# Weights times values in stick-breaking attention: three split products per head against one fp32 product on half of the array

## The chip, the cores and the metric

The kernel runs on one core of a Trainium2 chip. The metric is the device time of one execution in microseconds. Time before: median of three runs 3162.48 us (3160.17 to 3165.97).

## The reference

One step of a two-layer encoder: layer 0 uses latent attention, layer 1 stick-breaking attention, each followed by a squared-ReLU MLP. There are 1024 prompt frames, and 8 streams of 16 new frames with 128 cached ones. All tensors are fp32. What the change touches is the second mixer:

```
def sb_attend(q, q_pos, k, v, k_pos):
    z = einsum('bqhd,bkhd->bhqk', q, k) * (SB_HEAD_DIM ** -0.5)
    mask = (k_pos[None, :] < q_pos[:, None])
    log_keep = where(mask, log_sigmoid(-z), 0.0)
    suffix = cumsum(log_keep, axis=3, reverse=True) - log_keep
    a = where(mask, exp(log_sigmoid(z) + suffix), 0.0)
    return einsum('bhqk,bkhd->bqhd', a, v)

def sb_mixer(h, ...):            # 16 heads of 64
    qkv = (h @ w_in).reshape(B, S, 3, 16, 64)
    q, k, v = qkv[:, :, 0], qkv[:, :, 1], qkv[:, :, 2]
    out = attend_queries(sb_attend, ...)
    return out.reshape(B, S, 1024) @ w_o, k, v     # k and v are outputs too
```

## The kernel before, in words

**Number formats.** A product that must be exact is mostly made of three fp32r matmuls: each operand is split into a high part (a copy cast to fp32r) and a low part (the rest), and `product` (lines 72 to 76) issues high x high, high x low and low x high. [...]

**Stages.** Latent attention, MLP 0, `sb_input_stage` (projection to q, k, v; tiles named d_), `sb_attention_stage` (tiles named e_), then MLP 1. The change touches the two sb stages.

**sb_input_stage.** 60 tasks of 24 matmuls. For a v task of the prompt ScalarE casts the high half (L1770) and copies the rows for the output `new_p_sb_v` (L1776), VectorE makes the low half (L1805), and SyncE stores the rows (L1697) and both halves to the scratch tensor `sb_v` (L1712). Three tasks after the k tasks end, SyncE loads the operands of the first pair of heads (`load_queries_keys`, 12 transfers, `load_values`, 4 transfers).

**sb_attention_stage.** Heads go in 8 pairs, two pairs (32 steps) to a loop body: three passes of a hardware loop (`Fori`) and one written out. A step is one query tile of 128 rows of one head; `where(n)` gives pair, head and query tile. The order in a pair is q0, q1 of head 0, q0, q1 of head 1, then q2, q3 of each, and so on. Four steps are a group, two steps (one head) a unit. The chain of a step with q+1 key tiles:

- TensorE, `scores`: keys times queries, one or two chunks of up to 512 columns in four PSUM banks (L2301), and the mask (L2304).
- ScalarE, `weights`: two sigmoids of each chunk (L2101, L2103).
- VectorE, `scan`: a running product from the right (L2240). It frees the score bank.
- GpSimd, `weigh`: sigmoid times scan (L2190), the weights `take` (e_b).
- TensorE, `transposes`: each 128x128 block of weights is turned (L2357), up to four to a task, into one of three PSUM banks.
- ScalarE, `transposed_hi`: casts a task to the high part in `pt` (L2130); then VectorE, `transposed_lo`: writes the rest (L2272) and so frees the bank (`t_lo`).
- TensorE, `values`: after each unit, for each key tile, three matmuls of 256 columns into bank 7 (L74, L75, L76). The stationary operand holds the 64 value columns of the head beside 64 columns of zeros, so both heads of a pair add into one 128x256 result: head 0 fills partitions 0 to 63, head 1 the others.
- ScalarE, `output`: copies the result (L2137), SyncE stores it.

`pt` is two buffers of a high and a low part, one for each unit in turn. The order on each engine is the order of the code; all waits are on semaphores. On TensorE body step n runs a piece of the sample streams' attention if n+1 is odd (L2311 to L2336), `scores(n+4)`, `transposes(n+1)`, and, if n is odd, `values`. A task bank may be filled again when `emptied` holds. At the start of the stage VectorE zeroes parts of `pt` (L2222) and the 64 zero columns in each of the four value tiles (L2228); TensorE waits for all twelve of these (`const_done`).

Of the kernel before, what the change touches and what calls it, by code (L numbers as in the profile page):

```python
# [37 lines left out]
P = 128  # L38
# [1517 lines left out]
def sb_operands(nc, ctx, name):  # L1556

    q = ctx.enter_context(nc.sbuf_tensor(f"{name}_q", [P, 2, SEQ], F32R))
    k = [ctx.enter_context(nc.sbuf_tensor(f"{name}_k{s}", [P, 2, SEQ], F32R)) for s in "hl"]
    v = [ctx.enter_context(nc.sbuf_tensor(f"{name}_v{s}", [P, NPT, 3 * SB_DIM], F32R)) for s in "hl"]  # L1560
    return q, k, v


QK_LOADS, V_LOADS = 12, 4
# [17 lines left out]
def load_values(sp, scratch, operands, p, done):  # L1582

    for s in range(2):
        for a in range(2):
            sp.dma_start(f32(operands[2][s][:, :, 2 * a * SB_DIM:(2 * a + 1) * SB_DIM]),
                         scratch["sb_v"][s].rearrange("(t p) n -> p t n", p=P)[
                             :, :, bass.ds(p * 2 * SB_DIM + a * SB_DIM, SB_DIM)]).then_inc(done, 16)


def sb_input_stage(nc, io, scratch, h_t, sample):
# [22 lines left out]
    def to_halves(n):  # L1614

        kind, _, t = TASKS[n]
        return kind == "q" or (kind == "v" and t < NPT)
# [19 lines left out]
    with nc.cleanup_on_exit(), ExitStack() as ctx:  # L1637
# [45 lines left out]
        def _(sp):  # L1683
# [15 lines left out]
            def store_halves(n):  # L1699
                kind, g, t = TASKS[n]  # L1700
                for s in range(2):
# [4 lines left out]
                    elif kind == "k":  # L1706
# [3 lines left out]
                    else:  # L1710
                        dst = scratch["sb_v"][s, t * P:(t + 1) * P, (g - 4) * WIDTH:(g - 3) * WIDTH]
# [4 lines left out]
            for n in range(N):  # L1716
# [12 lines left out]
                if n == PRELOAD_AT:  # L1729
                    for u in range(3):  # L1730
                        half_stored[u].wait(sp, 32 * count(halves_stored, LAST, u))
                    done.wait(sp, LAST)
                    load_queries_keys(sp, scratch, first_pair, 0, first_in.sem)
                    load_values(sp, scratch, first_pair, 0, first_in.sem)
# [3 lines left out]
            first_in.wait(sp, 16 * (QK_LOADS + V_LOADS))  # L1738

        @block.scalar  # L1740
        def _(act):
# [19 lines left out]
            for n in range(N):  # L1761
# [5 lines left out]
                if to_halves(n):  # L1767
                    half_stored[n % 3].wait(act, 32 * count(halves_stored, n, n % 3))
                    width = COLS if kind == "q" else WIDTH
                    act.copy(half_st[n % 3][0][:, 0:width], task_bank(n)[:, 0:width]).then_inc(hi_out.sem, 1)  # L1770
# [22 lines left out]
        def _(dve):  # L1793
            for piece in range(0, PIECES, 2):
                weights_rest(dve, piece)
            for n in range(N):
                kind, g, t = TASKS[n]
                hi, lo = (x[:, 0:COLS if kind == "q" else WIDTH] for x in half_st[n % 3])
                if to_halves(n):
# [3 lines left out]
                    if to_rows(n):  # L1803
                        rows_out.wait(dve, count(to_rows, n + 1))
# [126 lines left out]
def sb_attention_stage(nc, io, scratch, first_pair, sample):  # L1931
# [7 lines left out]
    TURNS = S.count(TASKS, "prompt")  # L1939
# [3 lines left out]
    with nc.cleanup_on_exit(), ExitStack() as ctx:  # L1943
# [9 lines left out]
        pt = [[sb(f"e_pt{u}{s}", [P, NPT, GQ], F32R) for s in "hl"] for u in range(2)]  # L1953
        take = [sb("e_b0", [P, SEQ])]
        sample_rows(nc, ctx, "e")
        sb_operands(nc, ctx, "e_first")
        take += [sb(f"e_b{u}", [P, SEQ]) for u in range(1, 4)]
# [22 lines left out]
        t_done, t_hi, t_lo = signal("e_t"), signal("e_t_hi"), signal("e_t_lo", 3)  # L1980
# [24 lines left out]
        def emptied(pe, i, m):  # L2005
# [3 lines left out]
            if kind == "prompt":  # L2009
                t_lo.wait(pe, TURNS * i + S.count(before + 1, "prompt"))  # L2010
            elif kind == "values":
                smp_o.wait(pe, 2 * (S.SAMPLE_STEPS * i + S.count(before + 1, "values")))
            else:
                smp_out.wait(pe, 3 * S.SAMPLE_STEPS * i + S.count(before + 1, "keys", "scores", "turn"))

# [6 lines left out]
        def batch(i, f):  # L2022
            return 2 * i + f // 2

# [9 lines left out]
        def _(sp):  # L2034
# [22 lines left out]
            def body(i, last):  # L2057
                load_cache_k(i, 1, 2 * i + 1)
                for pair in range(2):
                    for g in range(4):  # L2060
# [5 lines left out]
                        if g == 0 and not (last and pair == 1):  # L2066
# [3 lines left out]
                            pv_done.wait(sp, S.UNITS * i + S.UNITS // 2 * pair)  # L2070
                            load_values(sp, scratch, operands[1 - pair], 2 * i + pair + 1, v_in.sem)
# [8 lines left out]
            sp.sem_inc(v_in.sem, 16 * V_LOADS)  # L2080
# [9 lines left out]
        def _(act):  # L2090
            o_done.start(act)
            smp_out.start(act)

# [24 lines left out]
            def transposed_hi(i, n):  # L2118
                unit, at = n // 2, (n % 2) * P
                for j, (kind, task) in enumerate(S.tasks(n)):  # L2120
                    m = S.before(n) + j
                    if kind == "values":
                        continue
# [4 lines left out]
                    pv_done.wait(act, S.UNITS * i + unit - 1)  # L2128
                    s0 = task[0][1]
                    act.copy(pt[unit % 2][0][:, s0:s0 + len(task), at:at + P],  # L2130
# [363 lines left out]
```

## Time and profile before

| | |
|---|---|
| median of three runs | 3162.48 us (3160.17 to 3165.97) |
| the profiled execution | 3161.52 us, span 3159.8 us |
| mean granted TensorE clock | 0.972 of full speed |
| busy: PE, DVE, ACT, POOL | 94%, 39%, 31%, 20% of the span |
| sb_input_stage | to about 1802 us |
| sb_attention_stage | about 1802 to 2225 us |

TensorE (PE) is the busiest engine nearly everywhere. [...] PEld is the load of the stationary operand, a record of its own.

### The profile page before, as it was taken

The page shows a single profiled execution, that of the slowest core. Times are in us where ns is not written, and L with a number is a line of the kernel's source. Part 1 is how long each engine was busy: PE and PEld are TensorE (multiplying, and loading weights), DVE is VectorE, ACT ScalarE, POOL GpSimd, SP SyncE. Part 2 cuts the span into 40 slices and gives each one's busy share as a digit, 9 for nine tenths or more (in the row PEclk, how much of TensorE's full clock was granted, in tenths as well). Part 3 has the DMA queues.
Part 4 walks back from the last instruction along what each step waited for, and adds up shares of the span by engine and source line. Part 5 has one row for each costly group of instructions (what it writes and reads, how often), then busy time and mean ns, then how long its engine had stood idle before and what let it go on. Part 6 is the DMA issues. An engine that isn't in the chain of part 4 may idle for free. (4 is left out here: it accounts for less than half of the span.)

```text
span 3159.8 us, 43537 instructions
## 1 busy us (share of the span) xinstructions
PE 2973.8 (94%) x16067; PEld 2648.4 (84%) x16067; DVE 1240.2 (39%) x1945; ACT 980.8 (31%) x2003; POOL 632.3 (20%) x484
## 2 busy tenths in 40 slices
PE   7979996999999999998999898899799999999998
PEld 6868885788999989997988777787679998899987
DVE  5556661442333323334101176767333332233324
ACT  4334442321122111223122265666322221122212
POOL 3100000121222112211121144444112211122111
PEclk9989997999999999999999999999899999999999
DMA  4211103411111111111345563643401111111111
GB/s 138 84 43 42 40 29 91 168 35 40 40 53 46 36 37 40 53 40 59 122 147 182 174 137 87 136 97 68 142 10 51 53 46 33 40 40 53 46 34 74
DMA packets 216173, 227.82 MB, mean 72 GB/s; under 512 B 50688, under 2 KB 174080, under 8 KB 216064
## 3 DMA queue, kind: packets, MB, share of 16 engines
q1 hardware_dynamic: 216064, 226.41, 24.5%
q8 instruction: 63, 1.03, 0.1%
q14 instruction: 46, 0.38, 0.0%
HBM read 170.36 MB, written 56.00 MB: 72 GB/s over the span
## 5 line engine op out<-in xcount | busy, mean ns | idle before, releaser
L1449 DVE TENSOR_TENSOR x<-m_ps,x 128x512 f32<-128x512 f32 x324 | 224.0, 691 | 670.4 <-PE m_ps L76 670.4
L1484 DVE TENSOR_TENSOR m_sq<-m_relu 128x384 f32<-128x384 f32 x192 | 171.1, 891 | 524.8 <-ACT m_relu L1388 524.8
L74 PE MATMUL m_ps<-h_h,m_up0h 128*128 128x384 f32 x768 | 258.8, 337 | 8.2 <-POOL m_up0l L1422 8.2
L75 PE MATMUL m_ps<-h_l,m_up0h 128*128 128x384 f32 x768 | 258.3, 336 | 0.0
L76 PE MATMUL m_ps<-h_h,m_up0l 128*128 128x384 f32 x768 | 258.3, 336 | 0.0
L74 PE MATMUL m_ps<-h_h,m_up1h 128*128 128x384 f32 x768 | 256.5, 334 | 0.0
L75 PE MATMUL m_ps<-h_l,m_up1h 128*128 128x384 f32 x768 | 256.5, 334 | 0.0
L76 PE MATMUL m_ps<-h_h,m_up1l 128*128 128x384 f32 x768 | 256.5, 334 | 0.0
L1388 ACT ACTIVATE m_relu<-m_ps 128x384 f32<-128x384 f32 x192 | 94.5, 492 | 513.9 <-PE m_ps L76 513.8
L2190 POOL TENSOR_TENSOR e_b<-e_b,e_r 128x128 f32<-128x128 f32 (+7 forms) x128 | 155.1, 1215 | 224.9 <-DVE e_r L2240 218.5
L1383 ACT CAST m_dn0h<-m_dn_raw 128x1024 fp32r<-128x1024 f32 x16 | 16.8, 1051 | 548.2 <-PE m_ps L76 548.2
L74 PEld LDWEIGHTS m_ps<-h_h,m_up0h 128*128 128x128 f32 x768 | 145.5, 190 | 9.2 <-POOL m_up0l L1422 8.6
L75 PEld LDWEIGHTS m_ps<-h_l,m_up0h 128*128 128x128 f32 x768 | 145.5, 189 | 0.5
L76 PEld LDWEIGHTS m_ps<-h_h,m_up0l 128*128 128x128 f32 x768 | 145.4, 189 | 0.0
L1429 POOL TENSOR_TENSOR m_dn0l<-m_dn_raw,m_dn0h 128x1024 fp32r<-128x1024 f32 x16 | 38.6, 2410 | 529.3 <-ACT m_dn0h L1383 529.3
L74 PEld LDWEIGHTS m_ps<-h_h,m_up1h 128*128 128x128 f32 x768 | 144.2, 188 | 0.0
L75 PEld LDWEIGHTS m_ps<-h_l,m_up1h 128*128 128x128 f32 x768 | 144.2, 188 | 0.0
L76 PEld LDWEIGHTS m_ps<-h_h,m_up1l 128*128 128x128 f32 x768 | 144.2, 188 | 0.0
L1422 POOL TENSOR_TENSOR m_up0l<-m_up_raw,m_up0h 128x1024 fp32r<-128x1024 f32 x32 | 76.7, 2396 | 320.2 <-ACT m_up0h L1376 320.2
L1488 DVE TENSOR_TENSOR m_ul<-m_sq,m_uh 128x384 fp32r<-128x384 f32 x192 | 113.2, 590 | 18.1
L1422 POOL TENSOR_TENSOR m_up1l<-m_up_raw,m_up1h 128x1024 fp32r<-128x1024 f32 x32 | 76.8, 2400 | 209.0 <-ACT m_up1h L1376 209.0
L2240 DVE TENSOR_TENSOR_SCAN e_r<-e_ps,e_zero 128x256 f32<-128x256 f32 (+3 forms) x128 | 108.6, 849 | 20.6 <-ACT e_ps L2103 18.2
(511 smaller groups left out, 7747.3 us busy)
## 6 DMA issues: line engine op xcount, KB each, us to landing
m_up_raw<-in_mlp_w_up SPq DMA_DIRECT2D x64, 512.0 KB, 4.6
m_dn_raw<-in_mlp_w_down SPq DMA_DIRECT2D x64, 512.0 KB, 3.6
h_raw<-scratch_oT SPq DMA_DIRECT2D x4, 1536.0 KB, 15.4
scratch_qr<-a_qrst SPq DMA_DIRECT2D x9, 512.0 KB, 3.4
a_x<-in_x_prompt SPq DMA_DIRECT2D x8, 512.0 KB, 4.9
b_qr<-scratch_qr SPq DMA_DIRECT2D x4, 1024.0 KB, 6.9
scratch_oT<-b_o SPq DMA_DIRECT2D x32, 128.0 KB, 1.7
new_p_sb_k<-d_rows SPq DMA_DIRECT2D x16, 256.0 KB, 2.1
```

The costliest lines, as they stand in the source:

```text
L74: pe.matmul(out, w[0], m[0], start=start, stop=False)
L75: pe.matmul(out, w[0], m[1], start=False, stop=False)
L76: return pe.matmul(out, w[1], m[0], start=False, stop=stop)
L1383: act.copy(w_dn[j][0][:], dn_raw[:]).then_inc(dn_hi.sem, 1)
L1388: act.activation(relu[n % 2][:], bank[:, (n + 2) % 4, 0:GROUP], ACT.Relu).then_inc(relu_done.sem, 1)
L1422: pool.tensor_tensor(w_up[j % 2][1][:], up_raw[:], f32(w_up[j % 2][0][:]), ALU.subtract).then_inc(up_lo.sem, 1)
L1429: pool.tensor_tensor(w_dn[j][1][:], dn_raw[:], f32(w_dn[j][0][:]), ALU.subtract).then_inc(dn_lo.sem, 1)
L1449: dve.tensor_tensor(x[:, t, cols], bank[:, 4 + n % 3, :], x[:, t, cols], ALU.add).then_inc(added.sem, 1)
L1484: dve.tensor_tensor(sq[n % 2][:], relu[n % 2][:], relu[n % 2][:], ALU.mult).then_inc(sq_done.sem, 1)
L1488: dve.tensor_tensor(u_t[1][:, j, cols], sq[n % 2][:], f32(u_t[0][:, j, cols]), ALU.subtract).then_inc(u_lo.sem, 1)
L2190: pool.tensor_tensor(b, b, rest[n % 2][:, SEQ - used + 1:SEQ + 1], ALU.mult).then_inc(weighted.sem, 1)
L2240: dve.tensor_tensor_scan(rest[n % 2][:, at:at + used][:, ::-1], keep[:, 0:used][:, ::-1], zero[:].broadcast_to([P, used]), start, ALU.mult ...
```

## The change

`pt` becomes four plain fp32 buffers (a unit each, so two groups), without high and low part. Each transposed task is copied once, by ScalarE or by VectorE in turns over the tasks (`copier`). The values are one fp32 tile of the pair's 128 columns, loaded with one transfer straight from the output `new_p_sb_v`; the scratch tensor `sb_v`, its halves and the zero columns go. `values` runs once a group, in two halves around the transposes of a step; each key tile has two fp32 matmuls with 64 stationary columns, head 0 into partitions 0 to 63 of bank 7 and head 1 into partitions 64 to 127. ScalarE's `output` now comes behind its copies of the step.

```diff
 def load_values(...):
-    for s in range(2):
-        for a in range(2):
-            sp.dma_start(f32(operands[2][s][:, :, 2 * a * SB_DIM:(2 * a + 1) * SB_DIM]),
-                         scratch["sb_v"][s]...)
+    sp.dma_start(operands[2][:], io["new_p_sb_v"][0, 0].rearrange("(t p) h c -> p t (h c)", p=P)[
+        :, :, bass.ds(p * 2 * SB_DIM, 2 * SB_DIM)]).then_inc(done, 16)
 # sb_input_stage
     def to_halves(n):
-        return kind == "q" or (kind == "v" and t < NPT)
+        return TASKS[n][0] == "q"
 # sb_attention_stage
-        pt = [[sb(f"e_pt{u}{s}", [P, NPT, GQ], F32R) for s in "hl"] for u in range(2)]
+        pt = [sb(f"e_pt{u}", [P, NPT, GQ]) for u in range(4)]
+        def copier(m):
+            return S.count(m, "prompt") % 2
+        def turned_rows(n, task):
+            s0, at = task[0][1], (n % 2) * P
+            return pt[n // 2 % 4][:, s0:s0 + len(task), at:at + P]
 # ScalarE
-            def transposed_hi(i, n):
+            def transposed(i, n):
-                    if kind == "values":
+                    if kind == "values" or kind == "prompt" and copier(m) == 1:
                         continue
-                    act.copy(pt[unit % 2][0][:, s0:s0 + len(task), at:at + P], ...)
+                    pv_done.wait(act, S.GROUPS * i + n // 4 - 1)
+                    act.copy(turned_rows(n, task), turned_in(m, task)).then_inc(t_out[0].sem, 1)
 # VectorE
-            for x in (*v[0], *v[1]):
-                dve.memset(f32(x[:, :, SB_DIM:2 * SB_DIM]), 0.0).then_inc(const_done.sem, 1)
-                    t_hi.wait(dve, TURNS * i + S.count(m + 1, "prompt"))
-                    dve.tensor_tensor(lo, task_bank(m)..., f32(hi), ALU.subtract).then_inc(t_lo.sem, 1)
+                    if kind == "prompt" and copier(m) == 1:
+                        t_done.wait(dve, TASKS * i + m + 1)
+                        pv_done.wait(dve, S.GROUPS * i + n // 4 - 1)
+                        dve.tensor_copy(turned_rows(n, task), turned_in(m, task)).then_inc(t_out[1].sem, 1)
 # TensorE
-            def values(i, unit):
-                for k, slot in order:
-                    done = product(pe, bank[:, 7, 0:GQ],
-                                   [x[:, k, a * SB_DIM:a * SB_DIM + P] for x in v[pair]],
-                                   [x[:, slot, :] for x in pt[unit % 2]], ...)
+            def values(i, g, half):
+                if half == 0:
+                    for u in range(2):
+                        t_out[u].wait(pe, TURNS * i + copies(ready, u))
+                for k, slot in order[middle:] if half else order[:middle]:
+                    for a in range(2):
+                        rows = slice(a * SB_DIM, (a + 1) * SB_DIM)
+                        done = pe.matmul(bank[rows, 7, 0:GQ], v[pair][:, k, rows], pt[2 * (g % 2) + a][:, slot, :],
+                                         start=k == last_q, stop=k == last_q - 1)
             def body(i, last):
                 for n in range(S.STEPS):
-                    step(i, n + S.VALUES_LAG, last)
-                    if n % 2 == 1:
-                        values(i, n // 2)
+                    m = n + S.VALUES_LAG
+                    step(i, m, last)               # without the transposes
+                    if n % 4 == 3:
+                        values(i, n // 4, 0)
+                    if not (last and m >= S.STEPS):
+                        transposes(i, m)
+                    if n % 4 == 3:
+                        values(i, n // 4, 1)
```

TensorE, second group of the first pair, before: the end of the fifth step's transposes and the start of head 1's values (e_pt1h and e_pt1l are the two parts of the turned weights, d_first_vh and d_first_vl those of the values).

```order
L2301 MATMUL e_ps<-d_first_kh,d_first_q 128x512
L2301 MATMUL e_ps<-d_first_kl,d_first_q 128x512
L95 REGISTER_ALU
L2357 MATMUL e_ps<-ident,e_b 128x128 x4
L95 REGISTER_ALU
L2357 MATMUL e_ps<-ident,e_b 128x128
L74 MATMUL e_ps<-e_pt1h,d_first_vh 128x256
L75 MATMUL e_ps<-e_pt1l,d_first_vh 128x256
L76 MATMUL e_ps<-e_pt1h,d_first_vl 128x256
```

TensorE at the same place now.

```order
L2301 MATMUL e_ps<-d_first_kh,d_first_q 128x512
L2301 MATMUL e_ps<-d_first_kl,d_first_q 128x512
L95 REGISTER_ALU x2
L2376 MATMUL e_ps<-e_pt,d_first_v 64x256 x4
L95 REGISTER_ALU
L2357 MATMUL e_ps<-ident,e_b 128x128 x4
L95 REGISTER_ALU
L2357 MATMUL e_ps<-ident,e_b 128x128
L2376 MATMUL e_ps<-e_pt,d_first_v 64x256 x4
```

The first half of the values now stands ahead of the transposes, directly behind the scores; both heads' products for a key tile follow each other, and the values of head 0, which had stood two steps earlier, are in the same two blocks.

VectorE at two steps of five and six key tiles, before (e_r is the scan).

```order
L2240 SCALAR_TENSOR_TENSOR e_r<-e_ps,e_r,e_zero 128x512
L2272 TENSOR_TENSOR e_pt0l<-e_ps,e_pt0h 128x4x128
L2272 TENSOR_TENSOR e_pt0l<-e_ps,e_pt0h 128x128
L95 REGISTER_ALU
L2240 SCALAR_TENSOR_TENSOR e_r<-e_ps,e_zero 128x384
L95 REGISTER_ALU x2
L2240 SCALAR_TENSOR_TENSOR e_r<-e_ps,e_r,e_zero 128x512
L2272 TENSOR_TENSOR e_pt0l<-e_ps,e_pt0h 128x4x128
L2272 TENSOR_TENSOR e_pt0l<-e_ps,e_pt0h 128x2x128
```

VectorE at the same two steps now.

```order
L2244 SCALAR_TENSOR_TENSOR e_r<-e_ps,e_r,e_zero 128x512
L95 REGISTER_ALU x2
L2273 COPY e_pt<-e_ps 128x128
L95 REGISTER_ALU
L2244 SCALAR_TENSOR_TENSOR e_r<-e_ps,e_zero 128x384
L95 REGISTER_ALU x2
L2244 SCALAR_TENSOR_TENSOR e_r<-e_ps,e_r,e_zero 128x512
L95 REGISTER_ALU
L2273 COPY e_pt<-e_ps 128x2x128
```

VectorE has one copy a step in place of two subtractions; the tasks of four tiles of these two steps went to ScalarE alone.

## Rows read from the trace of the kernel before

**Rows 1.** The page: busy time of each engine, share of the span.

```profile
PE 2973.8 (94%) x16067; PEld 2648.4 (84%) x16067; DVE 1240.2 (39%) x1945; ACT 980.8 (31%) x2003; POOL 632.3 (20%) x484
```

**Rows 2.** Busy time by stretch, the attention stage: PE, PEld, DVE, ACT, POOL, clock, DMA.

```profile
1805.00:1905.00 100.00, 92.58 (x613) 78.59 (x613) 70.99 (x108) 66.90 (x176) 46.52 (x47) 0.92 0.51 116
...
2105.00:2218.00 113.00, 102.47 (x713) 87.67 (x711) 77.54 (x120) 70.72 (x184) 47.08 (x45) 0.96 0.27 64
sum 413.00, PE 376.51 PEld 321.91 DVE 283.67 ACT 264.12 POOL 180.33; mean PE 94.13 PEld 80.48 DVE 70.92 ACT 66.03 POOL 45.08
```

**Rows 3.** Groups of instructions by line: values, busy and mean ns, idle before.

```profile
L74 PE MATMUL e_ps<-e_pt1h,e_second_vh 128*128 128x256 f32 x80 | 25.8, 323 | 4.8 <-DVE e_pt1l L2272 4.8
...
L75 PE MATMUL e_ps<-e_pt0l,d_first_vh 128*128 128x256 f32 x80 | 22.6, 282 | 0.0
```

**Rows 4.** Timeline of PE: start us, duration us. Values at full clock.

```profile
2007.74 0.28 PE L76 MATMUL e_ps<-e_pt0h,e_second_vl 128*128 128x256 f32 x1
2007.86 0.28 PE L74 MATMUL e_ps<-e_pt0h,e_second_vh 128*128 128x256 f32 x1
2007.98 0.28 PE L75 MATMUL e_ps<-e_pt0l,e_second_vh 128*128 128x256 f32 x1
```

**Rows 5.** Timeline of PE: four plain fp32 calls of 144 columns, eight records.

```profile
1858.77 1.14 PE L2320 MATMUL e_ps<-e_kT,e_qz 128*128 128x144 f32 x8
```

**Rows 6.** Timeline of PE and PEld: stationary loads beside matmuls.

```profile
1874.05 0.28 PE L76 MATMUL e_ps<-e_pt0h,e_second_vl 128*128 128x256 f32 x1
1874.05 0.19 PEld L74 LDWEIGHTS e_ps<-e_pt0h,e_second_vh 128*128 128x128 f32 x1
1874.41 1.04 PEld L2320 LDWEIGHTS e_ps<-e_kT,e_qz 128*128 128x128 f32 x8
```

**Rows 7.** Timeline of PE: 16 stationary rows between 128, and 16 stationary columns between 128.

```profile
1866.26 0.40 PE L2336 MATMUL e_ps<-e_wT,e_nv 16*128 16x32 f32 x2
1866.59 0.41 PE L2335 MATMUL e_ps<-e_wT,e_cv 128*128 128x32 f32 x2
1866.93 0.40 PE L2336 MATMUL e_ps<-e_wT,e_nv 16*128 16x32 f32 x2
...
2001.28 0.27 PE L2327 MATMUL e_ps<-ident,e_bs 128*128 128x128 f32 x1
2001.39 0.27 PE L2328 MATMUL e_ps<-ident,e_bs 128*16 128x128 f32 x1
2001.42 0.36 PE L2301 MATMUL e_ps<-d_first_kh,d_first_q 128*128 128x256 f32 x1
2001.62 0.28 PE L2301 MATMUL e_ps<-d_first_kl,d_first_q 128*128 128x256 f32 x1
```

**Rows 8.** Waits of PE in the stage: us in total, times, longest.

```profile
PE e_ps L2301 <- DVE e_r L2240: 12.0, 18, 3.1
PE e_ps L2301 <- DVE e_second_vl L2228: 10.0, 1, 10.0
PE e_ps L74 <- DVE e_pt1l L2272: 7.3, 12, 1.4
PE e_ps L2357 <- DVE e_pt0l L2272: 5.8, 16, 1.0
PE e_ps L74 <- DVE e_pt0l L2272: 4.7, 10, 0.6
PE e_ps L2357 <- DVE e_pt1l L2272: 4.5, 7, 0.9
```

**Rows 9.** Timeline from the last store of the input stage to the first scores.

```profile
1797.16 0.62 SPq L1697 DMA_DIRECT2D new_s_sb_v<-d_rows  x1
1802.06 0.34 SPq L2045 DMA_DIRECT2D e_ck<-in_cache_sb_k  x1
...
1804.82 0.48 DVE L2228 MEMSET e_second_vl<- 128x512 f32 x1
1805.36 0.58 PE L2301 MATMUL e_ps<-d_first_kh,d_first_q 128*128 128x256 f32 x1 [9.99 <-DVE e_second_vl L2228]
```

**Rows 10.** Timeline: one task's cast and subtraction, two scans.

```profile
2194.09 1.21 DVE L2240 TENSOR_TENSOR_SCAN e_r<-e_ps,e_zero 128x512 f32<-128x512 f32 x1
2195.41 1.28 DVE L2240 TENSOR_TENSOR_SCAN e_r<-e_ps,e_r,e_zero 128x512 f32<-128x512 f32 x1
2216.31 0.59 ACT L2130 CAST e_pt1h<-e_ps 128x512 fp32r<-128x512 f32 x1 [5.78 <-PE e_ps L2357]
2216.93 0.69 DVE L2272 TENSOR_TENSOR e_pt1l<-e_ps,e_pt1h 128x512 fp32r<-128x512 f32 x1 [0.73 <-ACT e_pt1h L2130]
```

More of the change, by code:

```diff
@@ L1705, in store_halves @@
                         src = src[:, 0:COLS]
-                    elif kind == "k":
+                    else:
                         a = PAIRS_W * (g - 2)
@@ L1768, in _ @@
                     half_stored[n % 3].wait(act, 32 * count(halves_stored, n, n % 3))
-                    width = COLS if kind == "q" else WIDTH
-                    act.copy(half_st[n % 3][0][:, 0:width], task_bank(n)[:, 0:width]).then_inc(hi_out.sem, 1)
+                    act.copy(half_st[n % 3][0][:, 0:COLS], task_bank(n)[:, 0:COLS]).then_inc(hi_out.sem, 1)
                 if to_sample(n):
@@ L1797, in _ @@
                 kind, g, t = TASKS[n]
-                hi, lo = (x[:, 0:COLS if kind == "q" else WIDTH] for x in half_st[n % 3])
+                hi, lo = (x[:, 0:COLS] for x in half_st[n % 3])
                 if to_halves(n):
@@ L1952, in sb_attention_stage @@
         q_st, k_tt, v = zip(*operands)
[L1953 to L1954 removed]
+        pt = [sb(f"e_pt{u}", [P, NPT, GQ]) for u in range(4)]
+        take = [sb(f"e_b{u}", [P, SEQ]) for u in range(3)]
         sample_rows(nc, ctx, "e")
         sb_operands(nc, ctx, "e_first")
[L1957 removed]
+        take.append(sb("e_b3", [P, SEQ]))
         rest = [sb(f"e_r{u}", [P, SEQ + 1]) for u in range(2)]
@@ L2009, in emptied @@
             if kind == "prompt":
-                t_lo.wait(pe, TURNS * i + S.count(before + 1, "prompt"))
+                copied_by(pe, i, before, before % TASKS)
             elif kind == "values":
@@ L2014, in emptied, with copies, copied_by @@
                 smp_out.wait(pe, 3 * S.SAMPLE_STEPS * i + S.count(before + 1, "keys", "scores", "turn"))
+        def copier(m):
+            return S.count(m, "prompt") % 2
+        def copies(m, u):
+            return (S.count(m, "prompt") + 1 - u) // 2
+        def copied_by(pe, i, m, place):
+            t_out[copier(place)].wait(pe, TURNS * i + copies(m + 1, copier(place)))
         def copied(engine, i, kind, f):
@@ L2092, in _ @@
             smp_out.start(act)
+            t_out[0].start(act)
             def weights(i, n):
@@ L2148, in body @@
                         step(i, m, last)
+                    if not (last and m >= S.STEPS):
+                        transposed(i, m)
                     if n % 4 == 3:
                         output(i, n // 4)
-                    if not (last and m >= S.STEPS):
-                        transposed_hi(i, m)
             const_done.wait(act, 4)
@@ L2218, in _ @@
             scanned_s.start(dve)
-            t_lo.start(dve)
+            t_out[1].start(dve)
             smp_o.start(dve)
-            for x in (*pt[0], *pt[1]):
-                dve.memset(f32(x[:, 0, 0:P]), 0.0).then_inc(const_done.sem, 1)
+            for x in pt:
+                dve.memset(x[:, 0, 0:P], 0.0).then_inc(const_done.sem, 1)
             for x in rest:
@@ L2381, in step @@
                     scores(i, n + S.AHEAD + 1)
-                if not (last and n >= S.STEPS):
-                    transposes(i, n)
             def body(i, last):
                 for n in range(S.STEPS):
-                    step(i, n + S.VALUES_LAG, last)
-                    if n % 2 == 1:
-                        values(i, n // 2)
-            const_done.wait(pe, 12)
+                    m = n + S.VALUES_LAG
+                    step(i, m, last)
+                    if n % 4 == 3:
+                        values(i, n // 4, 0)
+                    if not (last and m >= S.STEPS):
+                        transposes(i, m)
+                    if n % 4 == 3:
+                        values(i, n // 4, 1)
+            const_done.wait(pe, 8)
             for n in range(S.AHEAD + 1):
@@ L2395, in _ @@
                 step(0, n, False)
+                transposes(0, n)
             bodies(pe, body)
```

75 lines of the change are left out of this document (27 added, 48 removed).

## Prediction

> **What bounds the kernel now.** I read the page's busy shares first [rows 1]: TensorE 94%, everything else under 40%. Then the stretches of the attention stage, the only stage whose work changes much [rows 2]. In its 413 us TensorE has records for 376.5 us, VectorE for 283.7, ScalarE for 264.1, GpSimd for 180.3. So TensorE sets the time here too, but it is nearer to the others than in the MLP, and its clock is only 0.92 to 0.96 of full. The list of waits says what TensorE waits for [rows 8]: 22.3 us for the low part of the turned weights (7.3 + 4.7 before the values, 5.8 + 4.5 before a transpose that needs the bank), 12.0 us for the scan that frees a score bank, and once 10.0 us for the last memset at the start. The rest is matmuls behind matmuls, so a matmul that goes is time saved, as long as the next engine keeps up.
>
> The values are the largest single item. The groups by line [rows 3] show them as twelve groups of 80, from the costliest to the cheapest shown: 960 matmuls of 256 columns. Their durations (282 to 323 ns) overlap; the cost is the distance of two starts, 0.12 us at full clock [rows 4]. 960 x 0.12 = 115 us, more than a quarter of the stage.
>
> **Values on TensorE.** Removed: 960 x 0.12 = 115.2 us. Added: each pair has 20 key tiles over its four groups (2 + 4 + 6 + 8), two heads, eight pairs: 320 calls, and a plain fp32 call is two records: 640. What one costs at 256 columns is not in the trace, but four calls of 144 columns are, eight records in 1.14 us [rows 5]. The last one's duration is 0.286 us (all of this form are about that), so seven distances make 0.854 us, 0.122 each, 0.85 ns a column, twice the time of a column of the split form (0.12 us / 256 = 0.47 ns). At 256 columns that is 0.217 us a record. One after the other: 640 x 0.217 = 138.9 us, 23.7 us more than before: the change alone from three products to plain fp32 loses. It wins only if the two heads' matmuls, which use different halves of the array's columns, run beside each other. The order of the records is head 0 first and second record, head 1 first and second, so the second of one head can run beside the first of the other, and so on through the block: two at a time, 640 x 0.217 / 2 = 69.4 us. That is 45.8 us less than before. No row of this trace has two column halves in flight, so both ends stand: +24 and -46. I take -46. What speaks for it is that everything either half needs is its own: stationary columns, moving operand, partitions of bank 7.
>
> Can the stationary loads keep up? They are hidden now: the load of the next matmul starts with the matmul before it and is over in 0.19 us, and eight of the fp32 kind take 1.04 us, a distance of 0.12 or less [rows 6]. Two heads at a time want a load every 0.108 us, of half the columns. A load of all 128 columns would just not fit (0.12 against 0.108), one of 64 should.
>
> [...]
>
> **Changes of shape.** The values now stand in 64 blocks of half-width matmuls, entered and left 127 times or so. Two rows bound what that costs [rows 7]. Where 16 stationary rows alternate with 128, four fp32 records take 0.67 us (1866.26 to 1866.93) while eight with no change take 0.122 each, 0.49 for four: (0.67 - 0.49) / 2 = 0.09 us for a change, 11 us in all. Where 16 stationary columns stand between 128, two matmuls take 0.23 us (2001.39 to the second L2301 at 2001.62), 0.11 and 0.12, as without a change: nothing is lost. Columns are what changes here, so I take +3 us of 0 to 11. [...]
>
> **Copies.** A task of 512 columns takes ScalarE 0.59 us and then VectorE 0.69 [rows 10], in series with a gap between; only then may TensorE go on. Now one of them, in turns: the bank is free some 0.7 us earlier. The 10.3 us of waits of the transposes for a bank (longest 1.0) should nearly vanish: -8. Before the values the picture is mixed: the copy comes earlier, but the first half of a block now stands right behind one step's scores, no longer behind a step's transposes as well. From the last transpose to the end of the copy I count 0.17 + 0.59 + some 0.1 = 0.85 us; the scores between cover 0.3 to 1.0 us. About 0.4 us at each of 32 groups is 13 us, as the 12.0 us now. So 0. Bounds for both together: -18 to +8. VectorE loses 192 subtractions and gains 96 copies (a copy from PSUM is not in the trace in this size; nearest the subtraction's 0.69 or ScalarE's 0.59): it and ScalarE both lose close to half of that work, off TensorE's path.
>
> **Start of the stage.** The memsets of the zero columns go: four at a distance of 0.54 us, 2.2 us directly ahead of the first scores [rows 9]. The halves of the v tasks go too (16 casts, 16 subtractions, 32 stores) and the four value loads become one. In the input stage TensorE never waits for them, so they cost nothing there, but the queue is less behind: the last store was issued at 1797.16 and the next stage's first load at 1802.06. -2 us there, 0 to -3. Together -4.
>
> **What is late next.** With the values faster, VectorE comes near. Take the last group of a pair, two steps of seven and two of eight key tiles. VectorE has eight scans of up to 1.3 us and eight subtractions of up to 0.69 [rows 10], up to 15.9 us. TensorE has 48 values (5.8 us), 30 transposes at 0.11 (2001.28 to 2001.39 in [rows 7], 3.3 us), 7680 columns of scores at 0.47 ns (3.6 us), 12.7 us and a share of the samples' work. Now VectorE has four copies in place of the eight subtractions, up to 13.2 us, and TensorE 12.7 - 2.3 = 10.4 and the samples. So part of what the large groups gain (2.3 us x 8 pairs = 18 us) comes back as the wait for the scan, 12.0 us now [rows 8]. I add 10 us, of 0 to 18.
>
> **Sum.** -46 + 3 - 8 + 0 - 4 + 10 = -45 us, made against the profiled execution's 3161.5 us, 1.0 us below the median of the runs: 3117.5 after the 1.0 is added. I say 3118.
>
> **Rivals.**
> - *The halves don't overlap.* Every record waits for the one before it, as all matmuls of the trace do. For it: no row shows an overlap; a plain fp32 call is two records that follow each other in one half. Against it: nothing that the two halves share. +24 + 3 - 8 - 4, and no new wait for scans as TensorE stays the slowest, +2: +17, 3180. It decides from a record distance of 0.180 us, where 640 of them cost 115.2. This is the slower side.
> - *They overlap, but the loads show.* If each pair of records pays one load of 0.19 us, it takes 0.41, 320 x 0.41 = 131 us, +16 on the values and +7 in all: 3170. With half a load (64 columns), 0.31: 99 us, -16 and with the other terms -25: 3138.
> - *The clock.* At half clock the values lie 0.21 us apart in place of 0.12; this happens behind the samples' values, where TensorE does little. If half-wide matmuls or more waits bring the mean from 0.93 to 0.85 over the 370 us left, 370 x 0.08 = 30 us come back: 3148. Against it: records without a gap.
> - *The copies bind.* An engine that copies waits for the transpose itself, in order, ahead of the next scan or sigmoid. If each of 192 copies held a chain by 0.3 us more than now, +58 would undo the gain: 3160 or so, little for it as both engines have a third of the stage free.
>
> **How the numbers follow.** Forecast 0.60 (3118, own range 3095 to 3138), loads that show 0.10 (3138 to 3170), no overlap 0.17 (3180), clock 0.06 (3148), copies 0.03, something much slower 0.04. The range is 3095 to 3182. A measurement tells 0.2%, 6 us, from no change. Faster by more: 0.60 + 0.08 + 0.06 and half of the copies: 0.75. Slower: 0.17 + 0.04 = 0.21. Within: 0.04.
>
> **What will show it.** The fp32 values (L2376) as 640 records whose starts lie 0.108 us apart on average within a block: right; 0.217: the first rival; 0.15 to 0.2: the second. The first matmul behind a block a tenth of a us late: the change of shape costs. The stage's stretch from 1805 on near 370 us. PE's waits for the copies near 15 us with few before transposes, the wait for e_r at 15 to 30 us. DVE busy down by about 50 us in the stage, ACT by 35 to 40. The first scores 3 to 4 us earlier. The forecast is wrong if the distance is above 0.15, or if the distance is right and waits of TensorE grow by more than 25 us.

## The result, and the profile after

The changed kernel takes 3144.72 us (median of five runs, 3137.47 to 3147.97), the kernel before 3162.48 beside it (3158.77 to 3165.97): ratio 0.994, 95% interval 0.9922 to 0.9958. That is 18 us faster; 45 were forecast. The direction and the range held, the size didn't.

The page's busy shares, which answer to [rows 1]:

```profile
PE 2957.0 (94%) x15747; PEld 2585.5 (82%) x15747; DVE 1180.0 (38%) x1829; ACT 938.9 (30%) x1891; POOL 631.1 (20%) x484
```

The attention stage of the changed kernel as one stretch, then the kernel before over its whole stage (columns as in [rows 2]: start and end, length, busy time of PE, PEld, DVE, ACT and POOL, granted clock, DMA share, GB/s):

```profile
1807.00:2209.40 402.40, 359.30 (x2224) 260.24 (x2224) 239.01 (x336) 230.27 (x592) 180.18 (x176) 0.88 0.40 97
```

```profile
1805.40:2223.80 418.40, 381.71 (x2544) 326.91 (x2544) 283.85 (x432) 264.12 (x688) 180.33 (x176) 0.92 0.45 100
```

The stage is 16.0 us shorter. VectorE lost 45 us of work and ScalarE 34, about as forecast. TensorE's clock went from 0.92 to 0.88. Every stretch of its record is at 1.00 or at 0.50 of full speed, here and in the other 16 profiles, so the mean gives the time at half clock: 2 x 0.12 x 402 = 97 us, against 63 before (the record of the granted clock, which resolves it more finely than the two digits, has 98 and 63). At half clock the values of the kernel before lie 0.213 us apart in place of 0.12, and a block of four records of the changed kernel takes 1.05 us in place of 0.58. So work takes close to twice as long and costs half of its time extra. Counted over the matmuls that lie in these stretches that is 46.9 us, against 29.7 before: 17 more.

The values, in the timeline of PE (start, duration; answers to [rows 4]):

```profile
1906.50 0.33 PE L2357 MATMUL e_ps<-ident,e_b 128*128 128x128 f32 x1
1906.76 1.95 PE L2376 MATMUL e_ps<-e_pt,e_second_v 128*64 128x256 f32 x16
1908.64 0.65 PE L2311 MATMUL e_ps<-ident,e_ck 128*128 128x128 f32 x4
```

The values of the stage are 640 records for 320 calls, with 640 loads of 128x64 beside them (median 0.137 us): the 64 columns of e_second_v, which the call names first and the record last. Of the sixteen here the last is 0.38 us long: (1.95 - 0.38) / 15 = 0.105 us from one to the next on average. The row hides how: the records start in pairs 0.007 us apart, and a pair comes every 0.216 us. So the two column halves do run beside each other. But the block occupies 1.88 us to the next start, where 16 x 0.108 is 1.73. Blocks of 4, 8, 12 and 16 records take 0.58, 1.02, 1.45 and 1.88: 0.108 a record and 0.15 for the block. The blocks of the kernel before weren't free either: those of 6, 12, 18 and 24 records take 0.82, 1.53, 2.25 and 2.97 us at full clock, 0.12 a record and 0.10 for the block.

The waits of PE (us in total, times, longest), which answer to [rows 8]. "issue" is idle time for which the profile shows no releaser:

```profile
PE e_ps L2301 <- DVE e_r L2244: 26.3, 31, 3.6
PE e_ps L2376 <- DVE e_pt L2273: 7.4, 11, 1.2
PE e_ps L2376 <- issue: 7.0, 10, 1.1
PE e_ps L2301 <- SPq L2088: 5.8, 1, 5.8
PE e_ps L2376 <- ACT e_pt L2138: 1.4, 2, 0.8
```

The transposes wait for no bank any more (10.3 us before). The wait for the scan has doubled, and the values wait 15.8 us (12.0 before). The first scores come 5.8 us after the last matmul of the input stage (the L2088 row), 10.0 before [rows 8, 9]: -4.2, as forecast. A typical piece of the stage:

```profile
1861.68 0.44 PE L2301 MATMUL e_ps<-e_second_kh,e_second_q 128*128 128x384 f32 x1 [0.68 <-DVE e_r L2244]
1861.96 0.34 PE L2301 MATMUL e_ps<-e_second_kl,e_second_q 128*128 128x384 f32 x1
1863.33 0.65 PE L2376 MATMUL e_ps<-e_pt,e_second_v 128*64 128x256 f32 x4 [1.03 <-issue]
1863.91 0.87 PE L2357 MATMUL e_ps<-ident,e_b 128*128 128x128 f32 x3
1864.71 1.12 PE L2376 MATMUL e_ps<-e_pt,e_second_v 128*64 128x256 f32 x4
1865.77 0.64 PE L2335 MATMUL e_ps<-e_wT,e_cv 128*128 128x32 f32 x2
```

The same piece as stretches:

```profile
1859.00:1864.00 5.00, 3.29 (x23) 1.96 (x22) 4.02 (x6) 3.48 (x10) 2.25 (x3) 1.00 0.08 28
1864.00:1874.20 10.20, 10.20 (x38) 8.02 (x39) 3.48 (x7) 3.20 (x10) 2.58 (x3) 0.50 0.31 84
1874.20:1879.00 4.80, 4.52 (x31) 3.40 (x31) 4.36 (x6) 4.20 (x13) 2.64 (x2) 1.00 1.01 221
```

TensorE waits 0.68 us for a scan and 1.03 ahead of the first half of the values, then its clock is at half for 10.2 us, although in those it works without a gap. The samples' values (L2335, L2336) fall into them.

### The profile page after: what moved, and what is told of

It is laid out like the page before. It is cut to its first block and busy times, and to the rows that moved or that the text cites. A ratio compares the mean times of both kernels' runs of the same rounds, so it can differ in the third digit from the quotient of the medians.

```text
span 3145.2 us, 42670 instructions
## 1 busy us (share of the span) xinstructions
PE 2957.0 (94%) x15747; PEld 2585.5 (82%) x15747; DVE 1180.0 (38%) x1829; ACT 938.9 (30%) x1891; POOL 631.1 (20%) x484
## 3 DMA queue, kind: packets, MB, share of 16 engines
q1 hardware_dynamic: 186496, 213.82, 22.7%
q8 instruction: 62, 1.02, 0.1%
## 5 line engine op out<-in xcount | busy, mean ns | idle before, releaser
L1383 ACT CAST m_dn0h<-m_dn_raw 128x1024 fp32r<-128x1024 f32 x16 | 16.8, 1051 | 549.0 <-PE m_ps L76 549.0
```

The costliest lines, as they stand in the source:

```text
L1383: act.copy(w_dn[j][0][:], dn_raw[:]).then_inc(dn_hi.sem, 1)
```

## The experiments

All runs at a glance. Stage: from its first to its last matmul in the profiled execution. Clock: mean in the stage. Waits: TensorE's idle time in the stage ahead of scores (scans and key loads) / transposes / values; it is a little more than the lists of waits give, as these leave out idle times under 0.15 us. e11 and e12 also wait 8 and 15 us ahead of matmuls of the samples.

| kernel | median us | ratio to before (95%) | stage | clock | waits |
|---|---|---|---|---|---|
| before | 3162.48 | | 418.4 | 0.92 | 12.8 / 10.7 / 13.2 |
| changed | 3144.72 | 0.9922 to 0.9958 | 402.4 | 0.88 | 27.0 / 0 / 16.1 |
| e1_behind | 3110.09 | 0.9823 to 0.9850 | 368.5 | 0.92 | 27.4 / 1.3 / 5.9 |
| e2_ahead | 3124.01 | 0.9869 to 0.9899 | 386.4 | 0.91 | 32.7 / 0 / 13.9 |
| e3_serial | 3150.23 | 0.9952 to 0.9977 | 407.2 | 0.94 | 25.2 / 1.4 / 8.2 |
| e4_full | 3178.80 | 1.0034 to 1.0064 | 439.1 | 0.92 | 28.7 / 4.6 / 6.4 |
| e5_before_split | 3184.32 | 1.0052 to 1.0088 | 443.4 | 0.91 | 11.1 / 0.2 / 44.8 |
| e6_after_again | 3146.87 | 0.9929 to 0.9967 | 407.6 | 0.86 | 27.7 / 0 / 14.6 |
| e7_behind_act | 3128.16 | 0.9880 to 0.9916 | 389.5 | 0.89 | 41.8 / 1.3 / 1.9 |
| e8_behind_dve | 3112.95 | 0.9824 to 0.9860 | 377.1 | 0.91 | 20.8 / 5.5 / 7.3 |
| e9_pad | 3112.07 | 0.9830 to 0.9863 | 368.4 | 0.96 | 33.0 / 0 / 17.5 |
| e10_behind_pad | 3092.68 | 0.9769 to 0.9802 | 351.6 | 0.96 | 35.6 / 1.6 / 8.5 |
| e11_early_act | 3133.63 | 0.9886 to 0.9923 | 395.5 | 0.88 | 26.3 / 9.5 / 4.2 |
| e12_early_both | 3173.89 | 1.0029 to 1.0062 | 435.3 | 0.86 | 2.2 / 20.9 / 30.3 |
| e13_before_pad | 3134.81 | 0.9898 to 0.9931 | 392.4 | 0.98 | 12.6 / 11.9 / 17.6 |
| e14_late_pad | 3106.05 | 0.9811 to 0.9844 | 366.2 | 0.95 | 44.6 / 6.7 / 2.1 |
| e15_behind_pad_dve | 3092.42 | 0.9766 to 0.9802 | 352.1 | 0.97 | 28.3 / 6.6 / 8.1 |

**One block, behind or ahead of the transposes (e1_behind, e2_ahead).**

```diff
                     step(i, m, last)
-                    if n % 4 == 3:
-                        values(i, n // 4, 0)
                     if not (last and m >= S.STEPS):
                         transposes(i, m)
                     if n % 4 == 3:
+                        values(i, n // 4, 0)
                         values(i, n // 4, 1)
```

e2_ahead has both calls ahead of the transposes instead.

> The changed kernel with both halves of a group's values behind the transposes of the step, in one block. Theory 1, place: in the changed kernel the first half block stands ahead of the transposes, ScalarE and VectorE copy them in order ahead of the next sigmoids and scans, so scans come late. Then TensorE's waits for the scan fall from 26 us to 15 or less, those for copies before the values from 16 us (with the sequencer's own) to 5 or less, and the time falls by 12 to 25 us against the changed kernel (3144.7), to 3120 to 3133. Theory 2, cost of a block: in the changed kernel's trace a block of n records takes 0.108 n + 0.15 us; with 32 blocks in place of 64 that gives 5 us and no more: 3140. Theory 3, clock: half-wide matmuls themselves leave TensorE at half clock more often; nothing changes but the 5 us, and the half-clock time of the stage stays near 80 us.

> The changed kernel with both halves ahead of the transposes, in one block. Theory 1, place: copies and then scans come later by another half block (up to 1.9 us in the large groups): slower than the changed kernel by 10 to 25 us, 3155 to 3170, with more wait for the scan. Theory 2, cost of a block: as in the other order 5 us faster, 3140. Theory 3, clock: 3140 too.

The stage of e1_behind and its waits of PE:

```profile
1800.60:2169.20 368.60, 333.91 (x2224) 253.88 (x2224) 237.11 (x336) 229.63 (x593) 179.88 (x176) 0.92 0.43 105
```

```profile
PE e_ps L2301 <- DVE e_r L2244: 23.9, 24, 3.6
...
PE e_ps L2376 <- ACT e_pt L2138: 3.6, 6, 0.7
...
PE e_ps L2376 <- issue: 1.4, 3, 0.8
...
PE e_ps L2376 <- DVE e_pt L2273: 0.9, 2, 0.5
```

With the block behind the transposes 35 us come off the changed kernel. The waits ahead of the values fall from 16.1 to 5.9 us and the clock is back at 0.92. So where the values stand decides, far beyond the cost of a second block. It isn't by the way that theory 1 named: the scans were to come earlier, but TensorE's wait for them hardly moves (26.3 to 23.9 us), and the time lies below the ranges of all three theories. Ahead of the transposes the stage is 18 us longer than behind them, yet shorter than with the cut. That the cut is worse than either whole block was not expected; no theory had a time near the 3124 of e2_ahead.

**The two heads one after the other (e3_serial), and with the whole array (e4_full).** Both are e1_behind with head 0's products of a group first; e4_full has 128 stationary columns, two results and two copies of them in place of one.

```diff
-                for k, slot in order[middle:] if half else order[:middle]:
-                    for a in range(2):
+                for a in ([1] if half else [0]):
+                    for k, slot in order:
```

```diff
-                        done = pe.matmul(bank[rows, 7, 0:GQ], v[pair][:, k, rows], ...)
+                        done = pe.matmul(bank[:, 7, a * GQ:(a + 1) * GQ], v[pair][:, k, :], ...)
```

> As the block behind the transposes, but all products of head 0 and then all of head 1, so that neighbours lie on the same half of the array and can't run side by side. If the overlap is what the change wins by, the distance of two records goes from 0.108 to 0.213 us and the values cost 67 us more at full clock: 3185 to 3205. If something else sets the distance of 0.108, it stays. Theory 3 (half-wide matmuls let the clock fall): with twice the time in such matmuls the half-clock time of the stage grows well above 80 us. Theory 1 has the clock follow the idle time and the samples' small matmuls: it stays or falls.

> As the heads one after the other, but with both heads' 128 value columns stationary, so that each record uses the whole array (half of each result is not used; head 0's comes from one half of bank 7, head 1's from the other, with two copies). The same 640 records of 256 columns at 0.213 us. Theory 3: the half-clock time of the stage is clearly lower than with half-wide matmuls in the same order, by 30 us or more. Theory 1: both have the same half-clock time within 10 us, and the same time within 5 us.

The timeline of PE, the values of e3_serial (16 and 24 records), then of e4_full (16):

```profile
1974.96 2.86 PE L2376 MATMUL e_ps<-e_pt,e_second_v 128*64 128x256 f32 x16
...
1988.35 4.59 PE L2376 MATMUL e_ps<-e_pt,e_second_v 128*64 128x256 f32 x24
```

```profile
1991.41 3.62 PE L2377 MATMUL e_ps<-e_pt,e_second_v 128*128 128x256 f32 x16
1994.87 0.27 PE L2328 MATMUL e_ps<-ident,e_bs 128*128 128x128 f32 x1
```

Eight more records of the same halves cost 4.59 - 2.86 = 1.73 us, 0.216 each, and the whole array pays (1994.87 - 1991.41) / 16 = 0.216. So a half on its own gains nothing; the gain is the overlap of the two, and with most of it gone the kernel is at 3150 or, on the whole array, slower than before. Over the stage the values take 73.7 us at full clock in e1_behind, 116.4 in e3_serial, 139.6 in e4_full and 120.4 in the kernel before. The expectation for e3_serial was too high by 35 us or more, and that it would take the same time as e4_full was wrong, both mainly for one reason: a block of e3_serial is 0.7 us shorter than its records at 0.216, since (in the block of 16 above) the first four records of head 1 start beside the last four of head 0 (0.006 to 0.058 us behind one of them). Half-wide matmuls don't lower the clock either: e3_serial has 0.94, the full width 0.92.

**The cut in the kernel before (e5_before_split), and the changed kernel again (e6_after_again).** The edit of e5 (excerpt), with `values(i, unit, half)` taking half of the key tiles as in the changed kernel:

```diff
-                    step(i, n + S.VALUES_LAG, last)
-                    if n % 2 == 1:
-                        values(i, n // 2)
+                    m = n + S.VALUES_LAG
+                    step(i, m, last)               # without the transposes
+                    if n % 2 == 1:
+                        values(i, n // 2, 0)
+                    if not (last and m >= S.STEPS):
+                        transposes(i, m)
+                    if n % 2 == 1:
+                        values(i, n // 2, 1)
```

> The kernel before with its own three fp32r products per key tile, each unit's values cut in two halves around the transposes of the step; nothing else is changed. Theory 'the cut is what costs' (a block behind samples and transposes is what keeps TensorE busy and its clock up, whatever its matmuls are): the stage grows from 418 to 428 us or more and the time with half clock in it from 63 to 80 us or more; total 3172 or more. Theory 'only fast values can be cut badly' (the loss in the changed kernel comes from waits for copies that the short half-wide blocks no longer cover): the long blocks cover them, the stage stays within 5 us of 418, total 3157 to 3167.

> The changed kernel once more, unchanged, on the chip of the other runs here. If the 35 us more of half clock in its profile were an accident of one execution, this one has 60 to 70 us of half clock in the stage and a total near 3125. If they belong to the order of its work: 90 us or more again, stage near 402, total 3137 to 3148.

The cut alone costs the kernel before 23 us in the median and 25 in the stage, with its own matmuls. Its waits of PE:

```profile
PE e_ps L74 <- DVE e_pt1l L2272: 23.5, 28, 1.7
PE e_ps L74 <- DVE e_pt0l L2272: 21.2, 31, 1.6
PE e_ps L2301 <- DVE e_r L2240: 10.5, 11, 3.1
```

44.7 us ahead of the values, 12.0 before. So the cut costs, whatever is multiplied. Here most of it is waits (19 us more in all), and 8 us are the clock: 81 us at half clock in place of 63. And the low clock of the changed kernel is no accident: its second profile has 0.86.

**All copies on one engine (e7_behind_act, e8_behind_dve).**

```diff
-            return S.count(m, "prompt") % 2
+            return 0               # e7: ScalarE; e8 returns 1: VectorE
```

> One block of values a group behind the step's transposes, and all copies of turned weights on ScalarE (none on VectorE, which then has the scans alone and the samples). Theory A (the wait for the scan that frees a score bank, 27 us, comes from copies that stand ahead of the scans on VectorE): it falls to 15 us or less, but sigmoids come later on ScalarE; stage 355 to 365, total 3098 to 3106. Theory B (the scans wait for sigmoids, which stand behind copies on ScalarE): the wait grows to 35 us or more, total 3118 or more. Theory C (the wait comes from the faster TensorE alone and is nobody's copy): within 4 us of 27, total 3107 to 3114.

> The same with all copies on VectorE (192 in place of 96), none on ScalarE. Theory A: the wait for the scan grows from 27 to 40 us or more, total 3122 or more. Theory B: it falls below 20, total 3100 or less. Theory C: within 4 us of 27, total 3107 to 3114.

The waits of PE for scans and loads of keys, e7 and then e8:

```profile
PE e_ps L2301 <- DVE e_r L2244: 32.5, 30, 3.3
...
PE e_ps L2301 <- DMA d_first_kl<-scratch_sb_k: 8.8, 3, 3.6
```

```profile
PE e_ps L2301 <- DVE e_r L2244: 19.9, 38, 1.1
```

The wait ahead of scores goes 27 -> 42 with ScalarE alone and -> 21 with VectorE alone. The scans' part of it goes 23.9 -> 32.5 and -> 19.9; the rest of e7's growth is mostly loads of keys, 8.8 us in place of 3.0. So the copies on ScalarE delay the scans more than VectorE's 192 copies do; that they do it by holding the sigmoids is theory B's reading. Its numbers fit in part: e7 misses its 35 us, and e8 has its wait below 20 but not its total of 3100 or less. Only 4 us of the wait for scans hang on it, and VectorE alone gives them back ahead of transposes and values. e15_behind_pad_dve shows the same in the padded pair below, as was expected of it (wait 29 to 22 us, total 3090 to 3096): 29.1 -> 22.4 us for the scans, and no gain in the total.

**The samples' values with 128 rows (e9_pad, e10_behind_pad, e13_before_pad).** `new_v` gets 112 rows of zeros below its 16, and the second part of `wT` too, once at the start of the stage (excerpt):

```diff
-        new_v = sb("e_nv", [DEC_SEQ, S.PAIRS, P])
+        new_v = sb("e_nv", [P, S.PAIRS, P])
+            pool.memset(new_v[:], 0.0).then_inc(padded.sem, 1)
+            pool.memset(wT[:, 1, :], 0.0).then_inc(padded.sem, 1)
-                    last = pe.matmul(ps[:, cols], new_v[:, pair, :], wT[0:DEC_SEQ, 1, cols],
+                    last = pe.matmul(ps[:, cols], new_v[:, pair, :], wT[:, 1, cols],
```

> The changed kernel, but the samples' new values stand in 128 stationary rows, zeros below the 16, so that the products of L2335 and L2336 no longer alternate between 128 and 16 rows (0.168 us a record in the alternation, 0.11 without). Theory P (the alternation is the lull behind which the clock halves): the time with half clock in the stage falls from 98 to 112 us to 70 or less; the samples lose 64 records x 0.06 = 4 us or more besides; total 3115 to 3128. Theory Q (the clock goes with TensorE's waits and with where the short blocks stand): half clock 90 us or more again; 3136 to 3142.

> One block of values behind the transposes, and the same 128 rows for the samples' new values. Theory P: half clock in the stage falls from 60 to 40 us or less, total 3090 to 3098. Theory Q: half clock near 60, total 3103 to 3108, the 4 us of the records alone.

> The kernel before, with the samples' new values in 128 stationary rows as in the two kernels so changed. Theory P (it is the alternation of 128 and 16 rows that leads to half clock, and the change only makes each fall last longer): half clock in the stage falls from 63 to 30 us, stage near 392 to 400, total 3133 to 3142; the change measured between the two padded kernels is then -27 to -21 us against the -16 to -17 without. Theory R (the half clock of the kernel before has another source and only the changed order makes the alternation costly): half clock stays above 50 us, total 3153 to 3158.

The samples' values in e10_behind_pad, timeline of PE:

```profile
1856.95 0.39 PE L2340 MATMUL e_ps<-e_wT,e_nv 128*128 128x32 f32 x2
1857.17 0.39 PE L2339 MATMUL e_ps<-e_wT,e_cv 128*128 128x32 f32 x2
1857.40 0.39 PE L2340 MATMUL e_ps<-e_wT,e_nv 128*128 128x32 f32 x2
1857.62 0.39 PE L2339 MATMUL e_ps<-e_wT,e_cv 128*128 128x32 f32 x2
```

0.22 us for two records in place of 0.34 [rows 7]: over 128 pairs of records that is 15 us at full clock, more than the 4 that the expectations had, and the clock stays up behind them. The stages of the three padded kernels, e9_pad, e10_behind_pad and e13_before_pad:

```profile
1801.70:2170.10 368.40, 317.78 (x2224) 232.18 (x2224) 238.71 (x336) 230.20 (x592) 180.03 (x177) 0.96 0.43 105
```

```profile
1802.60:2154.30 351.70, 305.94 (x2224) 234.51 (x2224) 236.26 (x336) 229.33 (x592) 180.08 (x178) 0.96 0.46 110
```

```profile
1805.30:2197.70 392.40, 350.19 (x2544) 302.49 (x2544) 282.82 (x432) 263.62 (x688) 180.50 (x176) 0.98 0.48 107
```

Time at half clock, by the record: 63 -> 19 us in the kernel before, 98 -> 29 in the changed one, 60 -> 26 with one block behind. Theory P holds in that the samples' values are what the clock falls behind, and in the kernel before as well; its 26.0 us are 14 less in the samples' values, 17 less in all other matmuls by the clock, and 5 more of waits. The padding does two things, though: it ends the alternation of row counts, and it shortens 16 records in a row from 2.7 to 1.8 us. Which of the two keeps the clock up no run separates.

The record also shows two kinds of fall, beside the one at the start of the stage. In the kernel before 13 of 15 intervals at half clock begin during or behind the samples' values, with no wait of TensorE to speak of just ahead; two begin behind about 3 us of waits. In the changed kernel 7 of 14 begin behind 1.5 to 3.6 us of waits, and these seven hold 58 of the 98 us, since they last up to 10.2 us where the samples' values follow. With the padding none begins within 2 us behind the samples' values; those left in e9_pad (four), e10_behind_pad (four) and e13_before_pad (three) begin behind waits of 1.4 us or more.

Between padded kernels the change is worth 392.4 - 368.4 = 24.0 us of stage (22.7 in the medians), and with one block behind the transposes 40.7. e10_behind_pad is, with e15_behind_pad_dve, the fastest of all: 2.1% below the kernel before, 1.7% below the changed one.

**Sigmoids and scans one step earlier (e11_early_act, e12_early_both).** Both on e1_behind; eight e_b buffers of just the size needed take the place of four, and the wait for a free one follows them (excerpt).

```diff
 # ScalarE (e11, e12), and with scan in place of weights VectorE (e12)
-                if not (last and n + S.AHEAD >= S.STEPS):
-                    weights(i, n + S.AHEAD)
+                if not (last and n + S.AHEAD + 1 >= S.STEPS):
+                    weights(i, n + S.AHEAD + 1)
```

> One block behind the transposes; ScalarE now makes the sigmoids of a step before it waits for the transposes of the step that TensorE issues behind those scores (one step earlier; eight smaller e_b buffers in place of four make room). Theory B (the scans wait for sigmoids held behind ScalarE's copies): PE's wait for e_r falls from 24 to 27 us to 14 or less, total 3095 to 3103. Theory C (TensorE is simply faster than the chain of sigmoid and scan): within 4 us of now, 3106 to 3114.

> The same, and VectorE's scans one step earlier too, ahead of the copy that waits for those transposes. Theory B with VectorE's copies as a second cause: the wait for e_r falls to 8 us or less, total 3088 to 3097. If ScalarE's order alone holds the scans, no more than 2 us below the kernel with ScalarE's order changed alone. Theory C: 3106 to 3114.

Both lose, 24 and 64 us against e1_behind. The wait for the scan does go, to 4.6 us in e11, but into other waits:

```profile
PE e_ps L2301 <- DMA e_second_kl<-scratch_sb_k: 11.4, 4, 3.9
PE e_ps L2301 <- DMA d_first_kl<-scratch_sb_k: 10.2, 3, 4.3
...
PE e_ps L2357 <- ACT e_pt L2138: 5.4, 6, 1.2
PE e_ps L2301 <- DVE e_r L2244: 4.6, 10, 0.6
```

The sigmoids now wait for the scores, and the copies stand behind them. The clock falls too: 92 and 119 us at half clock in the stage, 60 in e1_behind. All three theories missed the total.

**The block one step later (e14_late_pad).** The block of e10_behind_pad stands behind the transposes of the next step:

```diff
-                    if n % 4 == 3:
+                    if n > 0 and n % 4 == 0 or n == S.STEPS - 1:
-                        values(i, n // 4, 0)
-                        values(i, n // 4, 1)
+                        values(i, (n - 1) // 4, 0)
+                        values(i, (n - 1) // 4, 1)
```

> Padded rows, one block of values a group, now behind the next step's transposes (one step later than in the padded kernel with the block behind). If what the place costs is the wait for the last copies: the 8.5 us of waits ahead of the values go, total 3082 to 3087. If TensorE only meets the same lateness elsewhere (the scans set the pace): the wait for e_r grows by about as much, total 3090 to 3096.

The waits ahead of the values fall from 8.5 to 2.1 us, as expected, but those ahead of the scores grow from 35.6 to 44.6 and those ahead of the transposes by 5. The total is 13 us above e10_behind_pad, more than either theory had. Of the growth, 8.6 us are waits for loads of keys (14.5 against 5.9 us by the lists of waits). Why these land later was not tried.

## Why the prediction was off

It forecast 41 us less in the stage and 4 at its start. Measured: 16.0 and 4.2. The stage can be taken apart. A matmul costs the distance of its start to the next one, less idle time; what half clock adds to that is a column of its own.

| kernel | matmuls at full clock | added by half clock | waits | stage |
|---|---|---|---|---|
| before | 352.1 | 29.7 | 36.7 | 418.4 |
| forecast | -43 | 0 | +2 | -41 |
| changed | 312.5 (-39.6) | 46.9 (+17.2) | 43.1 (+6.4) | 402.4 (-16.0) |
| e1_behind | 304.6 | 29.3 | 34.6 | 368.5 |
| e2_ahead | 307.4 | 32.2 | 46.8 | 386.4 |
| e5_before_split | 349.4 | 37.8 | 56.1 | 443.4 |
| e9_pad | 303.6 | 14.2 | 50.6 | 368.4 |
| e10_behind_pad | 293.6 | 12.4 | 45.7 | 351.6 |

Of the 25 us missed in the stage 17 are the clock, 4 the waits and 3 the matmuls. By the steps of the prediction:

- **Values, distance: right.** 0.108 us forecast, 0.105 to 0.108 measured; e3_serial and e4_full show 0.216 without the overlap. The first rival falls, and so does the second: the loads of 64 columns (median 0.137 us, of 128 columns 0.190 in e4_full) are hidden, since the records follow each other at that distance.
- **Values, changes of shape: right in size, by luck in part.** +3 was taken, of 0 to 11. 64 blocks at 0.15 us cost 9.6 us beside their records, but the blocks of the kernel before cost 0.10 us each, some 6 us that the prediction didn't price. The values went from 120.4 to 78.0 us at full clock, -42.4, where the forecast had -43; all other matmuls cost 2.8 us more.
- **Transposes' wait for banks: right.** -8 forecast, -10.7 measured.
- **What is late next: nearly right.** +10 forecast, +14 measured, inside the 0 to 18. That copies carry part of it (4 to 7 us by e8 and e15) was a rival at 0.03.
- **Wait ahead of the values: right as idle time, wrong in what it sets off.** "The first half of a block now stands right behind one step's scores" was seen and priced at 0, since the copies come earlier; the idle time went from 13.2 to 16.1 us. What was not priced is the cut itself. Against the one block of e1_behind it costs 34 us of stage: 17.6 by the clock, 8.5 of waits and 7.9 in the matmuls. Between the padded kernels it costs 16.8 (1.8, 4.9 and 10.0), in the kernel before 25.
- **The clock: the step that failed.** The sum has no term for it, so it stays as it was; as a rival it had 0.06 and 30 us, "against it: records without a gap". Measured: 98 us at half clock in place of 63, 17 us of time. Gaps there were: some 1.7 us just ahead of four stretches of 10.2 us at half clock in which the samples' values lie. It needed the cut (without it, e1_behind has 60 us at half clock) and the samples' values as they were (with padded rows, e9_pad has 29). How the cut brings it about is argued and not shown: e2_ahead waits 13.9 us ahead of its values and has only 68 us at half clock, e5_before_split waits 44.8 and has 81. So the total of the waits doesn't set it.

The 5.8 us by which the profiled execution reached the stage later than the one before (1801.2 against 1795.4) are scatter for the most part: 4.5 of them are there before the input stage begins, in identical code, and the second profile of the changed kernel has 1795.1.

A change with a single block behind the transposes comes close to what was priced: by the sum the stage of 418.4 us would have had 377, e1_behind has 368.5, with the clock's share as before and waits 4 us below the forecast's. The prediction's "near 370" came from a stretch of 413 us in place of the stage's 418.4, so that e1_behind meets it is luck.

## What to carry to other kernels

Price where a block of matmuls stands, not only what it costs. Here cutting each block in two cost 17 to 34 us of a stage of 400, by waits for copies, by dearer matmuls and by the clock, in shares that differ from kernel to kernel. The sum of busy and idle time doesn't show the clock's part, so look in the clock record for what stands behind a new wait. Thin matmuls in a row with alternating row counts were worth padding with zeros: 26 us in the kernel before, for two memsets.

## What was not expected of the hardware

- Plain fp32 matmuls into two column halves overlap in full: they start in pairs, a pair every 0.216 us at 256 columns (0.105 to 0.108 us a record), where one half alone (e3_serial) or the whole array (e4_full) needs 0.216 a record.
- A block of them costs 0.15 us beside its records, at any length from 4 to 16; a block of the three fp32r products in the kernel before costs 0.10, from 6 to 24.
- 256 matmul records of 32 columns, alternating between 128 and 16 rows, cost the kernel before 26 us of stage more than padded ones; padded, its time at half clock falls by 44 us.
- With the row counts equal such a record comes every 0.11 us (e10_behind_pad), alternating every 0.168 (the kernel before).
